# Level products of a linear attention issued alternately for two heads, and one clear for a range of semaphores

## The chip, the cores and the metric

One core of a Trainium2 chip runs the whole kernel. The core has a matrix engine (TensorE, PE in the profile), a vector engine (VectorE, DVE), a scalar engine (ScalarE, ACT), a general engine (GpSimd, POOL) and a queue engine (SyncE, SP), each with its own instruction stream; they meet at semaphores. The metric is the device time in microseconds of one execution, and the median of several executions is compared.

## The reference, cut to what matters

Two layers (DEPTH = 2) of a hybrid model work on two streams of 128 tokens each, a context stream and a sample stream, with 1024 channels. Each layer has a mixing half (gated linear attention with 4 heads, a convolution, a neighbourhood attention) and a mixture of 64 experts. The change touches the gated linear attention. Its part within a chunk is, for tokens i >= j of a chunk:

```
decay = jnp.exp(jnp.where(causal, diff, -jnp.inf))          # diff = bc_i - bc_j, bc = cumsum(log_a)
attn = jnp.sum(q[:, :, :, :, None, :] * k[:, :, :, None, :, :] * decay, axis=-1)
o_intra = jnp.einsum('bhnij,bhnjv->bhniv', attn, v)
```

It is computed forwards and, on the flipped sequence, backwards; both results are added, so each head needs attn for two directions. The head dimension is 64 (DK).

## The kernel before, in words

All weights are streamed from HBM through a ring of four slots; the activations stay in SBUF. The two layers are one hardware loop (`nc.Fori(0, DEPTH)`), whose body has two blocks: a large one with the work of all engines, and a small one in which GpSimd clears semaphores, so that the next pass of the loop can count them from zero again. At the end of a block all engines meet, and after the loop SyncE stores the two outputs.

In the linear attention the token by token matrix of a head is built from seven levels (LEVELS = 7). A level splits the 128 tokens into blocks and takes the products between the late half and the early half of each; scaled by decays relative to the middle of the block, it is one matrix product with 64 rows of contraction. The forward direction has an eighth product, the plain k times q, of which only the diagonal is used. The work is cut into 8 groups g per layer: stream st = g // 4, pair of heads a = g // 2 % 2, direction dr = g % 2. The two heads e = 0 and 1 of a pair lie in partitions 0 to 63 and 64 to 127 of the same tiles. A group goes through the engines like this:

- TensorE, `decays(g)` (L745): the sums of the log decays for the eight levels, into PSUM banks 0 and 1.
- ScalarE (L1136): their exponentials, into a tile E (shown as `h`, two buffers).
- VectorE for group 0, GpSimd for groups 1 to 7, `decayed` (L577, L579): E times q or k, into X (shown as `hT`, one buffer for each direction). It signals `X_ready`.
- TensorE, `pairs(g)` (L760, and L762 for the eighth product): X by X for each level, head 0 into banks 2 and 3, head 1 into banks 6 and 7. It signals `pair_shown` once for each head. A float32 product of the program is two MATMUL and two LDWEIGHTS instructions in the profile, so a head is 14 or 16 of each.
- VectorE, `combine(g)`: for each head a product of the eight (seven) levels with a mask into `tm` (L1353), which signals `masked`, a sum over the levels (L1358 forwards, L1360 backwards), and backwards an addition (L1361), which signals `att_ready`.
- TensorE, `outputs` (L774, L777): attention times v, after each second group.

Before head e of group g, TensorE waits until `masked` shows that VectorE has read the same head of the group before, since the banks are the same. The order on TensorE is written out by hand:

```
for g in range(8):
    pairs(g)
    if ADA_GLA + g < ADA_CHUNKS:
        ada_step(ADA_GLA + g)
    if g + 2 < 8:
        decays(g + 2)
    if g % 2 == 0 and g:
        outputs(g - 1)
outputs(7)
```

`ada_step` (L301, for g = 0, 1, 2) is a product of the modulation weights, with 32 columns of weights per instruction and four such products side by side in the array. After the eight groups follow the chunk states (L797, L799, L804) and the output projection (L812).

The clears are in the second block of the loop body. GpSimd walks over all 144 names and clears all but 15 of them, one instruction each (L1635). The 15 count on through the whole launch.

Of the kernel before, what the change touches and what calls it, by code (L numbers as in the profile page):

```python
# [29 lines left out]
DK = 64  # L30
# [20 lines left out]
LEVELS = 7  # L51
# [59 lines left out]
R_DW, R_DWB, R_LNG, R_LNB, R_ON, R_QN, R_KN, R_END = 0, 31, 32, 33, 34, 35, 36, 37  # L111


SIGNALS = """x_loaded c_loaded const_set const_step matrices c_sig c_step first_in0 first_in1
first_in2 first_in3 first_done first_kept first_bias bias_next small_in vec_in norm_in attn_in shared_in chunk_in0 chunk_in1 chunk_in2
gate_in0 gate_in1 gate_in2 gate_in3 down_in0 down_in1 down_in2 down_in3 act_step dve_step ada_done ada_kept bias_in square_done var_ready
root_ready mod_shown h_ready hT_shown hT_ready vec_shown vec_ready proj_done proj_kept z_shown la_log la_ready
conv_sig tap conv_ready convT_shown ctok_ready convB_shown conv_neg cact_ready pw_shown cat_conv nq_ready
kco_ready nT_shown nT_ready bias_ready scores_shown max_ready p_exp p_ready pT_shown pT_ready pv_shown cat_na
gg_sig decay_shown E_ready X_ready pair_shown masked att_ready o_shown go_ready goT_shown cat_gla st_pre  # L120
st_exp kd_ready st_shown st_kept mix_shown x_mid logits_shown scored g2_shown g2_kept stored y_out hs1 hs2 hs3 ordered tables_shown
tables_kept order_shown sorted_shown order_ready
rest1 rest2 chosen_ready counted places sh_gu sh_silu sh_act sh_turned sh_kept sh_done G_ready
S_ready X_shown X_kept gu_done silu_done act_done turned turn_kept Y_shown Y_kept scattered left_in left_base left_hot left_G left_Xs
# [16 lines left out]
def build(nc, A):  # L141
# [1 line left out]
        return nc.alloc_sbuf_tensor(name, shape, dt)  # L143


    s = {name: nc.alloc_semaphore(name) for name in SIGNALS}


    ring = sb("ring", [P, SLOTS, SLOT])
# [120 lines left out]
    def bank(b, lo=0, hi=512):  # L270
        return ps[:, b, lo:hi]
# [154 lines left out]
    def down(slot, j, half):  # L426
        return slot[:, 2 * KT * FF:SLOT].rearrange("p (j n) -> p j n", j=2)[:, j, 512 * half:512 * (half + 1)]
# [20 lines left out]
    with nc.Block() as block:  # L448
# [137 lines left out]
        def _(pe):  # L586
            mm = nc.tensor.matmul

            def show(n, st, b):

                for c in range(4):
                    last = mm(bank(b, P * c, P * (c + 1)), pick[:, c, st, :], ada[:, n, :], start=True, stop=True)  # L592
                return last
# [36 lines left out]
            for u, (c, c0, w, by_channel, st) in enumerate(UNITS_IN):  # L630
# [7 lines left out]
                for kt in range(KT):  # L638
                    if by_channel:
                        last = mm(ps[0:w, b, 0:STREAMS * P], wt[:, kt, :], hT[:, kt, :],  # L640
                                  start=(kt == 0), stop=(kt == KT - 1))
                    else:
                        last = mm(bank(b, 0, w), hT[:, kt, P * st:P * (st + 1)], wt[:, kt, :],  # L643
                                  start=(kt == 0), stop=(kt == KT - 1))
                last.then_inc(s["proj_done"], 1)
                if u == 3:
# [3 lines left out]
                    for c in range(2):  # L650
                        last = nc.tensor.transpose(bank(5, 64 * c, 64 * c + R_END), vec[:, P * c:P * (c + 1)],
                                                   ident[0:R_END, 0:R_END])
# [10 lines left out]
            for st in range(STREAMS):  # L663
                for c in range(2):
                    at = 256 * st + P * c
                    last = nc.tensor.transpose(bank(4, at, at + P), cacc[:, c, st, :], ident[:])
# [4 lines left out]
            for c in range(2):  # L671
                for st in range(STREAMS):
                    at = 256 * c + P * st
                    last = nc.tensor.transpose(bank(5, at, at + P), cTok[:, st, P * c:P * (c + 1)], ident[:])
# [4 lines left out]
            for o in range(2):  # L679
                for c in range(2):  # L680
                    last = mm(bank(4, 256 * o, 256 * (o + 1)), wpw[:, c, P * o:P * (o + 1)],
                              cacc[:, c, :, :].rearrange("p s t -> p (s t)"), start=(c == 0), stop=(c == 1))
# [10 lines left out]
            for a in range(PAIRS):  # L693
                last = nc.tensor.transpose(bank(6, P * a, P * (a + 1)), kvc[:, 0, P * a:P * (a + 1)], ident[:])
# [5 lines left out]
            for e in range(2):  # L700
                r = slice(DK * e, DK * (e + 1))
                for a in range(PAIRS):
                    last = mm(bank(2 + e, P * a, P * (a + 1)), qnT[r, a, 0:P], knT[r, a, 0:P], start=True, stop=True)
            last.then_inc(s["scores_shown"], 1)
            for e in range(2):
                r = slice(DK * e, DK * (e + 1))
                for a in range(PAIRS):
# [3 lines left out]
                    last = mm(bank(6 + e, 256 * a + P, 256 * (a + 1)), qnT[r, a, P:2 * P], kcT[r, a, :],  # L711
                              start=True, stop=True)
# [8 lines left out]
            for i, block_in in enumerate(blocks):  # L721
                last = nc.tensor.transpose(bank(i // 4, P * (i % 4), P * (i % 4 + 1)), block_in, ident[:])
# [3 lines left out]
            for e in range(2):  # L726
                for a in range(PAIRS):
# [6 lines left out]
                    last = mm(out1, kvc[:, 1, DK * hh:DK * (hh + 1)], pT[:, HEADS + 2 * i + 1, :],  # L734
                              start=False, stop=True)
# [13 lines left out]
            def pairs(g):  # L749

                st, a, dr = g // 4, g // 2 % 2, g % 2
                pe.wait_ge(s["X_ready"], g + 1)
                for e in range(2):
                    if g:
                        pe.wait_ge(s["masked"], 2 * (g - 1) + e + 1)
                    r = slice(DK * e, DK * (e + 1))
                    for lv in range(LEVELS + (dr == 0)):
                        out = bank((2, 6)[e] + lv // 4, P * (lv % 4), P * (lv % 4 + 1))
                        if lv < LEVELS:
                            last = mm(out, X[r, dr, lv, :], X[r, dr, lv, :], start=True, stop=True)  # L760
                        else:
                            last = mm(out, kT[r, a, P * st:P * (st + 1)], qT[r, a, P * st:P * (st + 1)],  # L762
                                      start=True, stop=True)
                    last.then_inc(s["pair_shown"], 1)

            def outputs(g):
                st, a = g // 4, g // 2 % 2
# [17 lines left out]
# [8 lines that stand above are left out]
# [5 lines left out]
            for dr in range(2):  # L798
                last = mm(bank(3, 256 * dr, 256 * (dr + 1)), suf[:, dr, :], la[:, 0, dr, :], start=True, stop=True)  # L799
            last.then_inc(s["st_pre"], 1)  # L800
            pe.wait_ge(s["kd_ready"], 1)
            for dr in range(2):
                for hh in range(HEADS):
                    last = mm(ps[0:DK, 6 + dr, DV * hh:DV * (hh + 1)], kd[:, dr, DK * hh:DK * (hh + 1)],  # L804
                              v[:, 0, DV * hh:DV * (hh + 1)], start=True, stop=True)
# [16 lines left out]
            for st in range(STREAMS):  # L822
                pe.wait_ge(s["go_ready"], st + 1)
                for hh in range(HEADS):
                    last = nc.tensor.transpose(bank(st, P * hh, P * (hh + 1)), gg[:, st, P * hh:P * (hh + 1)], ident[:])
# [13 lines left out]
            for st in range(STREAMS):  # L839
                for kt in range(KT):  # L840
                    last = mm(bank(2 + 4 * st, 0, EXPERTS), hT[:, kt, P * st:P * (st + 1)], wr[:, kt, :],
                              start=(kt == 0), stop=(kt == KT - 1))
                last.then_inc(s["logits_shown"], 1)
            for st in range(STREAMS):
                for half in range(2):
                    last = show(10 + half, st, G2_BANKS[2 * st + half])
# [17 lines left out]
            for st in range(STREAMS):  # L864
                last = mm(ps[0:EXPERTS, 2, 192:192 + EXPERTS], sel[:, st, :], ones[:, 0:EXPERTS], start=(st == 0),
                          stop=(st == STREAMS - 1))
# [5 lines left out]
            for st2 in range(STREAMS):  # L872
                nc.tensor.transpose(ps[0:EXPERTS, 6, P * st2:P * (st2 + 1)], place[:, st2, :], ident[:])
                last = nc.tensor.transpose(ps[0:EXPERTS, 6, P * (2 + st2):P * (3 + st2)],
                                           gate[:, st2, :], ident[:])
# [6 lines left out]
            for a in range(4):  # L882
                last = mm(bank(7, EXPERTS * a, EXPERTS * (a + 1)), tables[:, a, :], order, start=True, stop=True)
# [56 lines left out]
            for st in range(STREAMS):  # L940
                pe.wait_ge(s["sh_act"], st + 1)
                a_in = acts[:, st, :].rearrange("t (p j) -> t j p", j=2)
                for j in range(2):
                    last = nc.tensor.transpose(bank(4 + st, P * j, P * (j + 1)), a_in[:, j, :], ident[:])
# [3 lines left out]
            for st in range(STREAMS):  # L948
                pe.wait_ge(s["sh_kept"], st + 1)
                for half in range(2):  # L950
                    for j in range(2):
                        last = mm(bank(2 * st + half), sh_actT[:, st, P * j:P * (j + 1)], down(shared, j, half),
                                  start=(j == 0), stop=False, skip_group_check=True)
# [674 lines left out]
    with nc.Block() as block:  # L1628
        @block.gpsimd
        def _(pool):  # L1630
            for name in SIGNALS:
                if name not in ("stored", "const_step", "x_loaded", "c_sig", "c_step", "y_out", "c_loaded", "const_set",
                                "first_in0", "first_in1", "first_in2", "first_in3", "first_done", "first_kept",
                                "first_bias"):
                    pool.sem_clear(s[name])  # L1635
    layers.__exit__(None, None, None)


# [33 lines left out]
```

## Time and profile before

| what | us |
|---|---|
| median of 3 runs | 1714.33 |
| lowest, highest | 1712.02, 1715.88 |
| the profiled execution, its own time | 1718.69 |
| its span, from the first to the last instruction | 1717.1 |
| TensorE busy | 1497.6 |
| VectorE busy | 447.6 |
| ScalarE busy | 294.0 |
| GpSimd busy | 149.5 |

The profiled execution took 1.6 us more than its span and lies 4.4 us above the median. Busy time of TensorE is that of overlapping instructions in a pipeline, so it says that something was in the engine, and not that it ran at its peak. The granted clock of TensorE has two levels, shown as 1.00 (2.4 GHz) and 0.50 (1.2 GHz); a stretch with a number between them had both.

### The profile page before, as it was taken

How to read it: one execution, taken by the hardware profiler on the slowest of the kernel's cores; microseconds unless marked ns; L12 is line 12 of the kernel's file. 1: busy time of each engine (PE TensorE's matmuls, PEld its weight loads, DVE VectorE, ACT ScalarE, POOL GpSimd, SP SyncE). 2: the span in 40 equal slices, each digit the busy share in tenths (PEclk: the TensorE clock that was granted, in tenths of full speed). 3: DMA queues.
4: the chain of work that ended last, by engine and by line, in shares of the span. 5: the costliest groups of instructions: out<-in, count | busy, mean ns of one | idle time of the engine just before them, and what ended most of it. 6: DMA issues, size and time to landing. Idle time of an engine off the chain costs nothing. (4 is left out here: it accounts for less than half of the span.)

```text
span 1717.1 us, 28427 instructions
## 1 busy us (share of the span) xinstructions
PE 1497.6 (87%) x12120; PEld 797.8 (46%) x12121; DVE 447.6 (26%) x874; ACT 294.0 (17%) x489; POOL 149.5 (9%) x349
## 2 busy tenths in 40 slices
PE   4897889889898999899659879889899898999994
PEld 3655665634343344344246557564334343334431
DVE  1261684511111111111115219561111111111111
ACT  1313203500010101011023231251001010111110
POOL 3550240000000000000004106000000000000000
PEclk7998989899999999999969999889999999999997
DMA  7648910389999999999554594007999898989992
GB/s 253 228 134 313 334 58 6 139 339 419 367 422 389 421 390 391 390 421 403 215 185 171 175 386 184 7 1 292 403 406 384 368 413 362 416 365 392 404 421 105
DMA packets 109252, 509.56 MB, mean 297 GB/s; under 512 B 12864, under 2 KB 14652, under 8 KB 59196
## 3 DMA queue, kind: packets, MB, share of 16 engines
q1 hardware_dynamic: 108508, 506.52, 73.9%
q8 instruction: 101, 1.65, 0.4%
q0 software_dynamic: 384, 1.05, 0.3%
q14 instruction: 35, 0.29, 0.0%
q10 hardware_dynamic: 224, 0.06, 0.0%
HBM read 505.49 MB, written 2.10 MB: 296 GB/s over the span
## 5 line engine op out<-in xcount | busy, mean ns | idle before, releaser
L907 PE MATMUL ps<-ring,h 128*32 128x512 f32 x3328 | 394.4, 629 | 74.7 <-DMA ring<-in_exp_w_up 45.9
L907 PEld LDWEIGHTS ps<-ring,h 128*32 128x32 f32 x3328 | 118.2, 115 | 345.5 <-issue 345.3
L926 PE MATMUL ps<-ring,mid 128*32 128x512 f32 x1664 | 200.1, 598 | 3.1 <-DVE hT L1515 1.6
L933 PE MATMUL ps<-hT,mid 128*128 128x512 f32 x416 | 192.4, 605 | 1.6 <-DVE hT L1523 1.6
L893 PEld LDWEIGHTS ps<-tm,mid 128*128 128x128 bf16 x2496 | 144.4, 98 | 44.3 <-issue 43.1
L893 PE MATMUL ps<-tm,mid 128*128 128x128 bf16 x2496 | 156.9, 219 | 0.3
L1513 DVE TENSOR_TENSOR mid<-mid,ps 128x256 f32<-128x256 f32 x52 | 21.9, 421 | 470.4 <-ACT mid L1206 470.4
L933 PEld LDWEIGHTS ps<-hT,mid 128*128 128x128 f32 x416 | 74.7, 189 | 120.0 <-issue 116.5
L1515 DVE COPY hT<-ps 128x512 f32<-128x512 f32 x52 | 36.0, 691 | 329.0 <-PE ps L926 329.0
L1206 ACT ACTIVATE mid<-ps 128x256 f32<-128x256 f32 x52 | 19.9, 383 | 541.6 <-PE ps L907 541.6
L301 PE MATMUL ps<-ring,cs 128*32 128x128 f32 x1792 | 65.5, 309 | 46.7 <-DMA ring<-in_w_ada 46.7
L1604 POOL TENSOR_TENSOR ring<-ring,maskr 128x512 f32<-128x512 f32 x2 | 45.2, 22578 | 688.7 <-DMA ring<-in_cache_na_v 688.7
L643 PE MATMUL ps<-ring,hT 128*128 128x512 f32 (+1 forms) x256 | 96.5, 539 | 0.0
L1191 ACT COPY h<-ps 128x512 f32<-128x512 f32 x104 | 60.8, 585 | 177.5 <-PE ps L893 177.5
L301 PEld LDWEIGHTS ps<-ring,cs 128*32 128x32 f32 x1792 | 56.5, 125 | 53.0 <-DMA ring<-in_w_ada 38.9
L926 PEld LDWEIGHTS ps<-ring,mid 128*32 128x32 f32 x1664 | 43.6, 109 | 77.8 <-issue 64.0
L592 PE MATMUL ps<-ada,pick 128*128 128x128 f32 x384 | 52.3, 300 | 30.1 <-issue 18.4
L640 PE MATMUL ps<-hT,ring 128*128 128x256 f32 (+1 forms) x288 | 68.5, 400 | 2.2 <-ACT hT L1041 2.2
L643 PEld LDWEIGHTS ps<-ring,hT 128*128 128x128 f32 x256 | 48.6, 190 | 46.7 <-issue 45.0
L577 POOL TENSOR_TENSOR hT<-h,mid 128x64 f32<-128x64 f32 x196 | 57.3, 329 | 141.2 <-ACT h L1136 141.2
L592 PEld LDWEIGHTS ps<-ada,pick 128*128 128x128 f32 x384 | 51.0, 215 | 36.1 <-issue 30.0
L1208 ACT COPY mid<-ps 128x512 f32<-128x512 f32 x52 | 30.5, 586 | 186.1 <-PE ps L920 186.1
(276 smaller groups left out, 1256.9 us busy)
## 6 DMA issues: line engine op xcount, KB each, us to landing
ring<-in_exp_w_gate SPq DMA_DIRECT2D x128, 1024.0 KB, 10.5
ring<-in_exp_w_up SPq DMA_DIRECT2D x128, 1024.0 KB, 12.8
ring<-in_exp_w_down SPq DMA_DIRECT2D x128, 1024.0 KB, 13.8
ring<-in_w_ada SPq DMA_DIRECT2D x28, 2048.0 KB, 12.9
ring<-in_w_in SPq DMA_DIRECT2D x6, 2048.0 KB, 9.8
ring<-in_w_out SPq DMA_DIRECT2D x4, 2048.0 KB, 7.7
ring<-in_w_in SPq DMA_DIRECT2D x2, 3072.0 KB, 10.5
ring<-in_w_in SPq DMA_DIRECT2D x2, 2176.0 KB, 9.9
```

The source lines that it names most:

```text
L301: last = nc.tensor.matmul(out[32 * c:32 * (c + 1), :], cs[:, kt, :], w[:, kt, P * c:P * (c + 1)], start=(kt == 0), stop=(kt == KT - 1))
L577: last = tt(*views, ALU.mult)
L592: last = mm(bank(b, P * c, P * (c + 1)), pick[:, c, st, :], ada[:, n, :], start=True, stop=True)
L640: last = mm(ps[0:w, b, 0:STREAMS * P], wt[:, kt, :], hT[:, kt, :], start=(kt == 0), stop=(kt == KT - 1))
L643: last = mm(bank(b, 0, w), hT[:, kt, P * st:P * (st + 1)], wt[:, kt, :], start=(kt == 0), stop=(kt == KT - 1))
L893: last = mm(bank(X_bank, P * k, P * (k + 1)), hs[:, part, st, KT // 2 * half + k, :], onehot[:, st], start=(st == 0 and part == 0), stop=( ...
L907: last = mm(ps[first:first + TILE, 4, :], X_e[:, b, kt, first:first + TILE], gate_up(ring[:, slot, :], kt), start=(kt == 0), stop=(kt == K ...
L926: last = mm(ps[first:first + TILE, 7, :], turn[:, P * j + first:P * j + first + TILE], down(ring[:, slot, :], j, half), start=(j == 0), st ...
L933: last = mm(bank(2 * st + half), turn[:, FF + P * st:FF + P * (st + 1)], Y[:, 512 * half:512 * (half + 1)], start=False, stop=False, skip_ ...
L1191: return nc.scalar.copy(X_e[:, b, KT // 2 * half:KT // 2 * (half + 1), :], bank(6).rearrange("p (k n) -> p k n", n=P))
L1515: nc.vector.tensor_copy(Y[:, 0:512], bank(7)).then_inc(s["Y_kept"], 1)
L1604: nc.gpsimd.tensor_tensor(biasr, biasr, maskr[:].unsqueeze(1).broadcast_to([P, HEADS, P]), ALU.add)\
```

## The change

`pairs(g)` takes level by level and in each level head 0 and then head 1, where it took all levels of head 0 and then all of head 1. It waits once, for both heads of the group before, where it waited for each head ahead of its products. Head 0 is signalled behind its last product, which is the last but one of the group. The names of the 15 lasting semaphores are a list of their own, allocated first; the other 129 then have numbers in one unbroken range, and one instruction clears the range.

```diff
-    s = {name: nc.alloc_semaphore(name) for name in SIGNALS}
+    s = {name: nc.alloc_semaphore(name) for name in LASTING + SIGNALS}
+    numbers_of = [s[name].num for name in SIGNALS]
+    per_layer = range(min(numbers_of), max(numbers_of) + 1)
+    assert len(per_layer) == len(SIGNALS)
...
                 pe.wait_ge(s["X_ready"], g + 1)
-                for e in range(2):
-                    if g:
-                        pe.wait_ge(s["masked"], 2 * (g - 1) + e + 1)
-                    r = slice(DK * e, DK * (e + 1))
-                    for lv in range(LEVELS + (dr == 0)):
+                if g:
+                    pe.wait_ge(s["masked"], 2 * g)
+                for lv in range(LEVELS + (dr == 0)):
+                    for e in range(2):
+                        r = slice(DK * e, DK * (e + 1))
                         out = bank((2, 6)[e] + lv // 4, P * (lv % 4), P * (lv % 4 + 1))
                         if lv < LEVELS:
                             last = mm(out, X[r, dr, lv, :], X[r, dr, lv, :], start=True, stop=True)
                         else:
                             last = mm(out, kT[r, a, P * st:P * (st + 1)], qT[r, a, P * st:P * (st + 1)],
                                       start=True, stop=True)
-                    last.then_inc(s["pair_shown"], 1)
+                        if lv == LEVELS - (dr != 0):
+                            last.then_inc(s["pair_shown"], 1)
...
         def _(pool):
-            for name in SIGNALS:
-                if name not in ("stored", "const_step", "x_loaded", "c_sig", "c_step", "y_out", "c_loaded", "const_set",
-                                "first_in0", "first_in1", "first_in2", "first_in3", "first_done", "first_kept",
-                                "first_bias"):
-                    pool.sem_clear(s[name])
+            pool.sem_clear(per_layer)
```

## Rows read from the trace of the kernel before

**Rows 1.** The page: span and busy time of TensorE.

```profile
span 1717.1 us, 28427 instructions
PE 1497.6 (87%) x12120; PEld 797.8 (46%) x12121; DVE 447.6 (26%) x874; ACT 294.0 (17%) x489; POOL 149.5 (9%) x349
```

**Rows 2.** The clears, first layer and second: count, ns min/median/max, first and last start.

```profile
L1635 POOLq EVENT_SEMAPHORE_RANGE_CLEAR  x129: 37/38/47, 858.7 to 867.3; - x129
...
L1635 POOLq EVENT_SEMAPHORE_RANGE_CLEAR  x129: 37/38/47, 1703.9 to 1712.2; - x129
```

**Rows 3.** Timeline around the two ends of a layer: start, us, engine, line.

```profile
857.03 1.23 DVE L1558 TENSOR_TENSOR x<-x,tm 128x1024 f32<-128x1024 f32 x1
871.46 1.28 ACT L1034 ACT_TABLE_LOAD   x1 [27.55 <-issue]
...
1702.22 1.23 DVE L1558 TENSOR_TENSOR x<-x,tm 128x1024 f32<-128x1024 f32 x1
1712.73 0.36 SPq L1642 DMA_DIRECT2D out_y_prompt<-x  x1
```

**Rows 4.** The meeting after the clears, line L1636: ns, first and last start.

```profile
L1636 POOLq ALU_OP  x2: 35/40/45, 867.6 to 1712.5; - x2
...
L1636 PEldq COMPARE_BRANCH  x2: 79/1902/3724, 867.8 to 1712.8; - x2
```

**Rows 5.** Timeline, groups 0 and 1 of the first layer, TensorE and VectorE.

```profile
191.78 1.90 PE L760 MATMUL ps<-hT 64*128 64x128 f32 x16 [0.22 <-DVE hT L577]
...
193.52 0.27 PE L760 MATMUL ps<-hT 64*128 64x128 f32 x1
...
193.53 0.27 PE L762 MATMUL ps<-mid 64*128 64x128 f32 x1
193.63 1.39 PE L760 MATMUL ps<-hT 64*128 64x128 f32 x11
193.90 1.22 DVE L1353 TENSOR_TENSOR tm<-ps,maskf 128x1024 f32<-128x1024 f32 x1 [2.27 <-PE ps L762]
...
195.17 1.95 PE L301 MATMUL ps<-ring,cs 128*32 128x128 f32 x64
...
198.97 3.05 PE L760 MATMUL ps<-hT 64*128 64x128 f32 x28
...
200.90 1.09 DVE L1353 TENSOR_TENSOR tm<-ps,maskb 128x896 f32<-128x896 f32 x1 [0.46 <-PE ps L760]
```

**Rows 6.** What VectorE's L1353 waited for (us, times), then timeline, second layer's group 0.

```profile
  PE ps L762: 5.0, 4
  PE ps L760: 2.7, 4
...
1030.13 1.22 DVE L1353 TENSOR_TENSOR tm<-ps,maskf 128x1024 f32<-128x1024 f32 x1 [2.27 <-PE ps L762]
```

**Rows 7.** Timeline, groups 3 to 5 of the first layer.

```profile
218.82 1.09 DVE L1353 TENSOR_TENSOR tm<-ps,maskb 128x896 f32<-128x896 f32 x1
...
222.24 1.22 DVE L1353 TENSOR_TENSOR tm<-ps,maskf 128x1024 f32<-128x1024 f32 x1
...
225.50 1.23 DVE L1353 TENSOR_TENSOR tm<-ps,maskf 128x1024 f32<-128x1024 f32 x1
...
226.78 1.83 PE L760 MATMUL ps<-hT 64*128 64x128 f32 x14 [0.47 <-DVE tm L1353]
...
228.53 1.98 PE L745 MATMUL ps<-mb,mid 128*128 128x512 f32 x4
228.75 1.09 DVE L1353 TENSOR_TENSOR tm<-ps,maskb 128x896 f32<-128x896 f32 x1
```

**Rows 8.** Timeline, group 7; then windows (clock, DMA share, GB/s last).

```profile
239.92 3.35 PE L760 MATMUL ps<-hT 64*128 64x128 f32 x14 [1.35 <-DVE tm L1353]
...
238.00:240.00 2.00, 0.65 (x7) 0.46 (x5) 1.93 (x3) 0.00 (x0) 0.00 (x0) 0.92 0.00 0
...
256.00:258.00 2.00, 2.00 (x9) 1.35 (x8) 0.00 (x0) 0.91 (x1) 0.00 (x0) 0.81 0.00 0
```

More of the change, by code:

```diff
@@ L111 @@
 R_DW, R_DWB, R_LNG, R_LNB, R_ON, R_QN, R_KN, R_END = 0, 31, 32, 33, 34, 35, 36, 37
-SIGNALS = """x_loaded c_loaded const_set const_step matrices c_sig c_step first_in0 first_in1
-first_in2 first_in3 first_done first_kept first_bias bias_next small_in vec_in norm_in attn_in shared_in chunk_in0 chunk_in1 chunk_in2
+LASTING = """stored const_step x_loaded c_sig c_step y_out c_loaded const_set first_in0 first_in1 first_in2 first_in3
+first_done first_kept first_bias""".split()
+SIGNALS = """matrices bias_next small_in vec_in norm_in attn_in shared_in chunk_in0 chunk_in1 chunk_in2
 gate_in0 gate_in1 gate_in2 gate_in3 down_in0 down_in1 down_in2 down_in3 act_step dve_step ada_done ada_kept bias_in square_done var_ready
@@ L120 @@
 gg_sig decay_shown E_ready X_ready pair_shown masked att_ready o_shown go_ready goT_shown cat_gla st_pre
-st_exp kd_ready st_shown st_kept mix_shown x_mid logits_shown scored g2_shown g2_kept stored y_out hs1 hs2 hs3 ordered tables_shown
+st_exp kd_ready st_shown st_kept mix_shown x_mid logits_shown scored g2_shown g2_kept hs1 hs2 hs3 ordered tables_shown
 tables_kept order_shown sorted_shown order_ready
```

## The prediction

> **What bounds the kernel now.** I read the page first: the span is 1717.1 us and TensorE has something in it for 87% of that [rows 1]. This share says little of the change, which touches two short stretches of each layer. So I read those, each by its own view.
>
> The first is the end of a layer. The timeline has VectorE's last instruction at 857.03 for 1.23, so to 858.26, and the next work of any kind at 871.46, 13.2 us later; after the second layer it is 1703.45 to 1712.73, 9.3 us [rows 3]. The line of the clears fills this: 129 instructions from 858.7 to 867.3, and again from 1703.9 to 1712.2 [rows 2]. The meeting of the engines (L1636) follows at 867.6 and 1712.5 [rows 4]. Nothing runs beside the clears, so they are on the path in full. What remains of the first gap is the jump back to the start of the loop: the longer of TensorE's two branches on L1636 takes 3.72 us [rows 4], and the change leaves it.
>
> The second is the linear attention. The reader is to see who waits for whom in the timeline. VectorE's first mask product starts at 193.90, when head 0 of group 0 is there; in group 1 it waited 0.46 us for TensorE [rows 5]. The sum over both layers is 5.0 and 2.7, together 7.7 us; 2.27 of it in each layer is the first wait, before any product is there [rows 5, 6]. That leaves 7.7 - 4.5 = 3.2 us in which VectorE, in mid-chain, waited for a level product. From group 3 on it has no idle time noted before its mask products, and TensorE waits for VectorE (0.47 at 226.78) [rows 7]. So VectorE sets the pace here, at 6.8 us for a group (219.91 to 226.73, the ends of two second-head masks) [rows 7]. A faster TensorE can win 3.2 us in all, no more; a later one costs at once.
>
> **The clears.** 867.3 - 858.7 = 8.6 us and 1712.2 - 1703.9 = 8.3 us lie between the first and the last clear, 16.9 us together [rows 2]. The instruction that remains is of the same kind: the profile calls the single ones RANGE_CLEAR already, of 38 ns each, at a distance of 8.3 / 128 = 0.065 us. The unknown is what a range of 129 costs. Below, it is one instruction, and 16.9 us go. Above, it walks through its numbers: at 38 ns each that is 4.9 us a layer, 9.8 us back; at the old distance it would be all 16.9. I take the low end, since the same operation is nearest: -16.9. The clears may also have covered a fetch of instructions for what follows; the nearest row is the 3.7 us branch, which stands behind the clears uncovered as it is, so I put this at zero, with 3.7 us a layer as the upper end.
>
> **The alternation, if the two heads overlap.** 16 matmuls of one head take 1.90 us, the last of them 0.27, so they start (1.90 - 0.27) / 15 = 0.109 us apart [rows 5]. Do matmuls of different heads run at once? No row has a whole group in this order. But at the switch between heads in group 0, one of head 1 starts at 193.52 and one of head 0 at 193.53 [rows 5]: 0.01 apart, each with its own weights, into different banks. And the 64 instructions of L301, issued in turn over four column parts, start (1.95 - 0.27) / 63 = 0.027 us apart, a quarter of 0.109 [rows 5]. I take full overlap: a group then needs 1.9 us, not 3.5, and head 0 is complete in the same slot as when it ran alone.
>
> The Trainium skill (TensorE: Matmul & The Clock Gate, "LDWEIGHTS (loading the stationary operand)") speaks against: the load time goes by the 128 columns, whatever the rows. If loads of the two heads queued for one path, nothing would overlap, and the sum would be that of the first rival. Its Part 3 lets loads overlap where row groups differ, and the pair at 193.52 agrees with that.
>
> Now the wait. Both heads start behind the second mask of the group before. Call its end T. TensorE starts at T + 0.05 (226.73 to 226.78) [rows 7]. From the start of a group to VectorE's mask product is 1.93 us with seven levels (198.97 to 200.90) and 2.12 with eight (191.78 to 193.90) [rows 5], so head 0 is usable at T + 1.98 and T + 2.17. VectorE comes free for it at T + 2.02 behind a forward group (226.73 to 228.75) and T + 2.33 behind a backward one (219.91 to 222.24) [rows 7]. The sum over levels hides the products, by 0.04 and 0.16 us. The cover is thin, so I don't take all of the 3.2 us: 0.1 us at some 12 of the 14 later groups stays, and the term is -2.0 (from 0 to -3.2).
>
> Behind the waiting instruction are ada_step, decays(g+2) and outputs on TensorE, and behind them ScalarE and GpSimd. They are not later: they stood behind the same mask, that of the second head, before, with one head's products (1.8 us) still to come, and now two heads' in the same time.
>
> **TensorE's clock.** This is the cost I did not expect at first. Before, a group gave TensorE two bursts of products and one of decays (1.98), with a short pause such as 0.47 [rows 7]. After, from group 3 on, it has 1.9 + 2.0 us of work, at times 0.5 more, in 6.8, then a pause of 2.4 to 2.9 us directly ahead of the next products; ahead of group 7, which has no decays before it, about 3.3. The granted clock fell from 1.00 to 0.50 in the slice from 238 to 240, around a pause of 1.35 ahead of group 7's head 1, and came back only in that from 256 to 258 [rows 8]. So the clock can fall here, ahead of groups 4 to 7. At 1.2 GHz the 14 products of a head take 3.35 us [rows 8] against 1.83 [rows 7]: +1.5, uncovered, while before this befell only head 1 of group 7, behind 2 us of other work. Groups 0 to 3 have the 2 us of an ada_step or short pauses. At most 4 groups x 2 layers x 1.5 = 12 us; at least 0. The pauses lie between one that the clock did not mind (0.47) and more than twice the one around which it fell, yet before it fell once a layer only. I take half: +6.
>
> **Sum:** -16.9 - 2.0 + 6.0 = -12.9 us. The profiled execution's own 1718.69 (span 1717.1 and 1.6 around it) becomes 1705.8. It lies 4.4 above the median of 1714.33, and the same difference gives 1701.4.
>
> **Rivals.** (1) *The heads don't overlap.* Against it stands the pair at 193.52; for it, that only two or so of a group's slots are seen doubled. Head 0's last product would then come 14 slots later with eight levels, 1.52 us, and 12 with seven, 1.30. VectorE waits 1.52 in group 0, 2.17 + 1.52 - 2.33 = 1.36 in the three other forward groups, 1.98 + 1.30 - 2.02 = 1.26 in the four backward ones: 10.6 a layer, 21.2 in all, in place of the 3.2. With -16.9 that is +1.1: 1715.4. If group 7 is at 1.2 GHz its slots double, about 3.3 more a layer: 1722, slower. It decides where head 0 comes 1.2 us late per group or more.
>
> (2) *The clear walks its range.* +9.8 on the forecast: 1711.2. For it, nothing but that no row has a wide range.
>
> (3) *The clock holds.* No +6: 1695.4; with every wait gone 1694.2. (4) *It falls ahead of all eight groups.* +6 more, and the waits stay: 1709.4.
>
> (5) *A fetch comes out from behind the clears.* Up to 7.4: 1708.8.
>
> **How the numbers follow.** Overlap and a cheap clear, with the clock anywhere between (3) and (4), 0.78; rival 1, 0.12, of it two thirds slower; rival 2, 0.06, on the border; rival 5, 0.04. The range from 1694 to 1709 is that of (3) to (4), with some 0.8 in it. A change within 0.2% (3.4 us) can't be told from none here. Faster by more: 0.78 + 0.04 + half of 0.06 = 0.85; within, 0.07; slower, 0.08.
>
> **What the profile will show.** One RANGE_CLEAR a layer, about 0.04 us, and gaps of 4.6 and 1.0 us where 13.2 and 9.3 were. Starts of head 0 and head 1 in pairs, a group's 32 matmuls in about 2 us; at 3.5 rival 1 holds. VectorE's waits for L760 and L762 beyond the first 2.27 under 1 us a layer at clock 1.00, and waits of 1.5 us exactly where the clock is 0.50. The forecast is wrong if the clear is long, if the pairs don't coincide, or if the clock falls never or always.

## The result, and the profile after

| what | before | after |
|---|---|---|
| median, us | 1713.17 (4 runs) | 1692.01 (4 runs) |
| lowest, highest | 1710.96, 1715.88 | 1689.78, 1698.42 |
| the profiled execution, its own time | 1718.69 | 1698.42 |
| its span | 1717.1 | 1696.8 |

The ratio is 0.9882, with a 95% interval from 0.985 to 0.9914: 20 us faster, between 15 and 26. The forecast was 12.9 us faster, and the median lies 2 us below its range. Two repeats of the same kernel gave 0.9902 (0.9883 to 0.9921) and 0.9894 (0.987 to 0.9917), so about 17 to 18 us. Among the runs of the experiments below, one execution of one_wait (3825 us) and two of the kernel before (2224 and 1987 us) were far slower than all others of the same kernel; they are left out of the ratios and of one_wait's median.

The clears first. These are the rows of the page, of the line of the clear and of the branch behind it, which answer to [rows 1, 2, 4], then those of the timeline at the two ends of a layer, which answer to [rows 3].

```profile
span 1696.8 us, 28171 instructions
PE 1480.1 (87%) x12120; PEld 781.1 (46%) x12121; DVE 446.0 (26%) x874; ACT 293.9 (17%) x489; POOL 149.8 (9%) x349
...
L1637 POOLq EVENT_SEMAPHORE_RANGE_CLEAR  x2: 740/740/740, 862.3 to 1691.2; - x2
...
L1638 PEldq COMPARE_BRANCH  x2: 79/1790/3500, 863.5 to 1692.4; - x2
```

```profile
860.57 1.22 DVE L1564 TENSOR_TENSOR x<-x,tm 128x1024 f32<-128x1024 f32 x1
866.98 1.28 ACT L1040 ACT_TABLE_LOAD   x1 [19.54 <-issue]
...
1689.50 1.23 DVE L1564 TENSOR_TENSOR x<-x,tm 128x1024 f32<-128x1024 f32 x1
1692.41 0.36 SPq L1644 DMA_DIRECT2D out_y_prompt<-x  x1
```

A clear takes 0.74 us and not 0.04. The gap from 861.79 to 866.98 is 5.2 us where it was 13.2, that from 1690.73 to 1692.41 is 1.7 where it was 9.3: 8.0 and 7.6 us less, together 15.6. The longer branch at the end of the loop body takes 3.50 us, where it took 3.72.

Next the level products: TensorE in the timeline of the first layer, groups 0, 1, 4, 5, 6 and 7.

```profile
193.54 1.83 PE L765 MATMUL ps<-hT 64*128 64x128 f32 x28 [0.23 <-DVE hT L582]
195.17 0.42 PE L767 MATMUL ps<-mid 64*128 64x128 f32 x4
...
200.31 1.83 PE L765 MATMUL ps<-hT 64*128 64x128 f32 x28 [0.93 <-DVE tm L1359]
...
219.84 3.33 PE L765 MATMUL ps<-hT 64*128 64x128 f32 x28 [2.61 <-DVE tm L1359]
222.90 0.63 PE L767 MATMUL ps<-mid 64*128 64x128 f32 x4
...
228.18 1.83 PE L765 MATMUL ps<-hT 64*128 64x128 f32 x28 [2.30 <-DVE tm L1359]
...
234.52 1.83 PE L765 MATMUL ps<-hT 64*128 64x128 f32 x28 [2.59 <-DVE tm L1359]
...
241.28 3.36 PE L765 MATMUL ps<-hT 64*128 64x128 f32 x28 [3.18 <-DVE tm L1359]
```

28 matmuls in 1.83 us, where 28 took 3.05 [rows 5]: the heads run side by side, (1.83 - 0.27) / 27 = 0.058 us apart. The pause ahead of the products is 0.2 to 0.9 us in the early groups and 2.3 to 3.2 from group 4 on, and in groups 4 and 7 the same 28 take 3.33 and 3.36 us. In groups 5 and 6 they take 1.83 us, behind pauses of 2.30 and 2.59 us, so the pause alone does not decide it. The windows say why; they answer to [rows 8], and the third number from the end is the clock.

```profile
218.00:220.00 2.00, 0.16 (x2) 0.19 (x4) 1.90 (x4) 0.29 (x1) 1.80 (x7) 0.98 0.92 389
220.00:222.00 2.00, 2.00 (x20) 2.00 (x22) 1.97 (x2) 0.00 (x0) 2.00 (x8) 0.50 0.03 8
222.00:224.00 2.00, 2.00 (x18) 1.61 (x16) 0.42 (x2) 0.00 (x0) 0.93 (x3) 0.67 0.00 0
224.00:226.00 2.00, 1.88 (x8) 0.97 (x6) 1.97 (x2) 0.53 (x1) 0.00 (x0) 1.00 0.00 0
...
254.00:256.00 2.00, 0.52 (x2) 0.11 (x1) 0.75 (x3) 0.60 (x1) 0.00 (x0) 0.99 0.00 0
```

The clock falls as group 4's products start, and is back within 4 us. VectorE pays for it: these are its waits of over 0.2 us for a level product, first layer and then second (the 2.27 of the second layer's first group is not shown), and below them the sums over both layers, which answer to [rows 6].

```profile
195.66 1.23 DVE L1359 TENSOR_TENSOR tm<-ps,maskf 128x1024 f32<-128x1024 f32 x1 [2.27 <-PE ps L767]
...
223.58 1.23 DVE L1359 TENSOR_TENSOR tm<-ps,maskf 128x1024 f32<-128x1024 f32 x1 [1.58 <-PE ps L767]
...
244.71 1.09 DVE L1359 TENSOR_TENSOR tm<-ps,maskb 128x896 f32<-128x896 f32 x1 [1.61 <-PE ps L765]
...
1051.27 1.23 DVE L1359 TENSOR_TENSOR tm<-ps,maskf 128x1024 f32<-128x1024 f32 x1 [0.75 <-PE ps L767]
...
1065.36 1.23 DVE L1359 TENSOR_TENSOR tm<-ps,maskf 128x1024 f32<-128x1024 f32 x1 [0.96 <-PE ps L767]
...
1073.37 1.09 DVE L1359 TENSOR_TENSOR tm<-ps,maskb 128x896 f32<-128x896 f32 x1 [1.62 <-PE ps L765]
...
  PE ps L767: 8.2, 7
  PE ps L765: 3.2, 2
```

The waits of 0.46 in group 1 and their like are gone, and five of 0.75 to 1.62 us have come. In sum 11.4 - 4.5 = 6.9 us behind the two first waits, where it was 3.2: +3.7. And yet the stage as a whole did not get longer. I measure it from VectorE's first mask product to the mean square of the second stream behind the attention (L542 before, L547 after): in the first layer from 193.90 to 265.46, which is 71.6 us, and now from 195.66 to 266.42, 70.8. In the second it is 71.6 and 71.2 us. The products of the chunk states behind the groups show part of it, before and after:

```profile
253.54 3.51 PE L804 MATMUL ps<-mid,ring 128*64 128x128 f32 x16 [1.54 <-DVE ring L1371]
...
265.46 0.17 DVE L542 TENSOR_SCALAR sm<-sm 128x4 f32<-128x4 f32 x1
```

```profile
256.06 1.96 PE L810 MATMUL ps<-mid,ring 128*64 128x128 f32 x16 [1.54 <-DVE ring L1377]
...
266.42 0.17 DVE L547 TENSOR_SCALAR sm<-sm 128x4 f32<-128x4 f32 x1
```

They run at 2.4 GHz now, as the clock is back at 254 and not at 256 to 258 [rows 8]. The part on the prediction shows that this earlier return is not bound to the alternation.

### The profile page after: what moved, and what is told of

Same layout as the page of the kernel before. It is cut to its first block and busy times, and to the rows that moved or that the text cites. A ratio compares the mean times of both kernels' runs of the same rounds, so it can differ in the third digit from the quotient of the medians.

```text
span 1696.8 us, 28171 instructions
## 1 busy us (share of the span) xinstructions
PE 1480.1 (87%) x12120; PEld 781.1 (46%) x12121; DVE 446.0 (26%) x874; ACT 293.9 (17%) x489; POOL 149.8 (9%) x349
## 5 line engine op out<-in xcount | busy, mean ns | idle before, releaser
L306 PE MATMUL ps<-ring,cs 128*32 128x128 f32 x1792 | 69.0, 320 | 44.7 <-DMA ring<-in_w_ada 44.7
## 6 DMA issues: line engine op xcount, KB each, us to landing
ring<-in_w_ada SPq DMA_DIRECT2D x28, 2048.0 KB, 13.2
```

The costliest lines, as they stand in the source:

```text
L306: last = nc.tensor.matmul(out[32 * c:32 * (c + 1), :], cs[:, kt, :], w[:, kt, P * c:P * (c + 1)], start=(kt == 0), stop=(kt == KT - 1))
```

## The experiments

Each has a profile, and each but clear_sizes was timed beside the kernel before on the same chip. In the table the stage is the one defined above, of both layers added, in the one execution that was profiled; in the kernel before it is 143.1 us, in the changed kernel's first profile 142.0.

| kernel | median, us | ratio to before (95%) | stage, us |
|---|---|---|---|
| clear_only | 1695.1 | 0.9905 (0.9887 to 0.9923) | 141.7 |
| alt_only | 1706.8 | 0.9977 (0.9958 to 0.9995) | 139.8 |
| renumber | 1712.1 | 1.0006 (0.9988 to 1.0023) | 143.0 |
| both_again | 1694.0 | 0.9902 (0.9883 to 0.9921) | 142.2 |
| both_third | 1691.5 | 0.9894 (0.987 to 0.9917) | 140.8 |
| one_wait | 1696.7 | 0.9908 (0.9883 to 0.9933) | 145.2 |
| hybrid | 1689.1 | 0.9879 (0.9846 to 0.9911) | 135.7 |
| filler | 1682.3 | 0.9831 (0.9801 to 0.9861) | 135.6 |
| late_decays | 1684.0 | 0.9833 (0.9802 to 0.9864) | 135.9 |
| late_again | 1683.4 | 0.9842 (0.9819 to 0.9866) | 137.3 |
| late_old | 1689.8 | 0.9883 (0.986 to 0.9905) | 143.8 |
| clear_sizes | 1694.2 (one execution) | none | 139.6 |

**clear_only.** The clears as changed, the level products as before.

```diff
-                if g:
-                    pe.wait_ge(s["masked"], 2 * g)
-                for lv in range(LEVELS + (dr == 0)):
-                    for e in range(2):
+                for e in range(2):
+                    if g:
+                        pe.wait_ge(s["masked"], 2 * (g - 1) + e + 1)
+                    for lv in range(LEVELS + (dr == 0)):
...
```

> The one range clear and the new list of lasting semaphores, with the level products in the old order. Theory A (the change is the clears, the alternation is near zero): the profile of the changed kernel has gaps of 9.3 and 1.7 us between the last VectorE instruction and the next work at the two ends of a layer... worked out from VectorE's starts on either side, 8.0 and 7.6 us less than before, so -15.6 us, and this kernel is 15.6 us faster than before, to 2 us. Theory B (the alternation wins several us of its own, also outside its stage): the same -15.6 here, and the rest of the 21 us in the next kernel. Theory C (something beside the clears themselves, such as where code or semaphores lie, moves the time): clearly more than 15.6 here.

The first of the two gaps is 5.2 us, not 9.3; the differences of 8.0 and 7.6 us are right. The kernel is 16.2 us faster (13 to 19), as the gaps say: theory A's 15.6 lies within, and theory C is not needed. Theory B expects the same here.

**alt_only.** The kernel before with the new `pairs(g)`.

```diff
-                for e in range(2):
-                    if g:
-                        pe.wait_ge(s["masked"], 2 * (g - 1) + e + 1)
-                    for lv in range(LEVELS + (dr == 0)):
+                if g:
+                    pe.wait_ge(s["masked"], 2 * g)
+                for lv in range(LEVELS + (dr == 0)):
+                    for e in range(2):
...
```

> The alternation and its single wait, with the 129 single clears. Theory A: between +1 and -3 us, since the waits that it removes (3.2 us) and those that it adds at 1.2 GHz (about 7 us in the profile) and an earlier return of the clock behind the groups nearly cancel. Theory B: -5 us or more. In the profile the pairs start together and the waits of about 1.6 us stand where the granted clock is 0.50.

3.9 us faster, with an interval from 0.9 to 7.2. This is between the two theories. In the profiled execution the stage was 139.8 us, one of the short ones. Of its waits at the low clock one is the 1.6 us expected (1.62) and three are less, 0.42, 0.98 and 1.39. The one of 0.42 is in group 4 of the first layer, where the fall of the clock caught only a part of the products: 28 of them took 2.14 us.

**renumber.** The new order of allocation, but 129 single clears and the old products.

```diff
-            pool.sem_clear(per_layer)
+            for name in SIGNALS:
+                pool.sem_clear(s[name])
```

> Only the semaphore numbers change: the lasting ones are allocated first, and the 129 are cleared one by one in the old order of products. Theories A and B: no difference, within 2 us; a difference here is what two equal programs differ by. Theory C: some us faster.

No difference, which refutes theory C.

**both_again, both_third.** The changed kernel, unaltered.

> The changed kernel once more, on the same chip as its parts. Theory A: 16 to 18 us faster than before, the sum of the two parts, and the 21 us of the first four runs were partly scatter. Theory B: 20 us or more faster.

> The changed kernel again: 16 to 20 us faster than before, the range of its two measurements so far.

16.8 and 18.1 us faster. On the chip of its parts it was 1.1 us faster than clear_only, and it is not clear of it; the alternation is worth little, and these runs do not tell its share from nothing. The two parts alone add up to 16.2 + 3.9 = 20.1 us, which the intervals also allow.

**clear_sizes.** The changed kernel with eight redundant clears of 1 to 96 semaphores.

```diff
             pool.sem_clear(per_layer)
+            for n in (1, 2, 4, 8, 16, 32, 64, 96):
+                pool.sem_clear(range(per_layer[0], per_layer[0] + n))
```

> The changed kernel with eight more clears behind its own, of 1, 2, 4, 8, 16, 32, 64 and 96 semaphores of the same range, so that the profile shows the time of a clear against its length. If the engine walks its range, the times rise in a line from 0.04 us for one to 0.74 for 129, which is 0.0055 us a semaphore; if 0.74 us is what any wide clear costs, they are all near 0.74 but the first. The whole kernel is about 2 x 2 us slower by the first, 2 x 6 by the second.

The line of the added clears (count, then ns min/median/max), in three narrow windows: those of 1 and 2, of 16 and 32, of 64 and 96 semaphores. The last row is the clear of all 129.

```profile
L1639 POOLq EVENT_SEMAPHORE_RANGE_CLEAR  x2: 44/44/45, 860.3 to 860.3; - x2
...
L1639 POOLq EVENT_SEMAPHORE_RANGE_CLEAR  x2: 113/156/200, 860.6 to 860.7; - x2
...
L1639 POOLq EVENT_SEMAPHORE_RANGE_CLEAR  x2: 372/458/545, 861.0 to 861.4; - x2
...
L1637 POOLq EVENT_SEMAPHORE_RANGE_CLEAR  x2: 740/740/740, 859.5 to 1684.9; - x2
```

The time grows in a line with the range, as it would if the clear walks it: 372 - 200 = 172 ns for 32 semaphores more, 545 - 372 = 173 for the next 32, 5.4 ns each. One or two take 44 to 45 ns. From the start of the last VectorE instruction to the end of the span it is now 8.95 us, against 7.30 in the changed kernel, so the eight clears, 1.4 us a layer by themselves, are on the path too.

**one_wait.** The changed kernel, with head 0 and then head 1 behind the one wait.

```diff
-                for lv in range(LEVELS + (dr == 0)):
-                    for e in range(2):
+                for e in range(2):
+                    for lv in range(LEVELS + (dr == 0)):
```

> As the changed kernel, but with the heads one after the other behind the one wait: the wait without the alternation. If both heads run at once in the alternation, then a group costs TensorE 3.5 us again here and VectorE waits 0.1 to 0.9 us in groups 1 to 3 as before or more, while in groups 4 to 7 head 0 is ready as early as in the alternation; the longer burst leaves a shorter pause, so fewer falls of the clock: between 0 and 3 us slower than the changed kernel by the first, 3 us faster by the second if the clock holds. Theory A expects them near equal.

VectorE's waits in its first layer, in the timeline:

```profile
193.71 1.23 DVE L1358 TENSOR_TENSOR tm<-ps,maskf 128x1024 f32<-128x1024 f32 x1 [2.27 <-PE ps L767]
...
200.71 1.09 DVE L1358 TENSOR_TENSOR tm<-ps,maskb 128x896 f32<-128x896 f32 x1 [0.44 <-PE ps L765]
...
207.71 1.22 DVE L1358 TENSOR_TENSOR tm<-ps,maskf 128x1024 f32<-128x1024 f32 x1 [0.20 <-PE ps L767]
...
215.16 1.09 DVE L1358 TENSOR_TENSOR tm<-ps,maskb 128x896 f32<-128x896 f32 x1 [0.88 <-PE ps L765]
```

Behind the first they are 0.44, 0.20 and 0.88 us, in groups 1, 2 and 3. In the kernel before they are 0.46 [rows 5], 0.20 and 0.89. So it is the alternation that removes them. In groups 4 to 7 no wait is left in this layer, with the same one wait ahead of the products: here, with the clock at 2.4 GHz, the wait alone cost nothing. In its second layer the clock fell at 1048.5 for 6.8 us, and the waits there are some 5 us behind the first, which makes the stage the longest of all, 145.2 us. The whole kernel can't be told from the changed one (0.9908 against 0.9882 to 0.9902).

**hybrid.** Groups 0 to 3 alternate behind one wait, groups 4 to 7 go as before.

```diff
+                levels = LEVELS + (dr == 0)
+                if g < 4:
+                    if g:
+                        pe.wait_ge(s["masked"], 2 * g)
+                    order = [(lv, e) for lv in range(levels) for e in range(2)]
+                else:
+                    order = [(lv, e) for e in range(2) for lv in range(levels)]
+                for lv, e in order:
+                    if g >= 4 and lv == 0:
+                        pe.wait_ge(s["masked"], 2 * (g - 1) + e + 1)
...
```

> As the changed kernel, but only groups 0 to 3 alternate, behind one wait; groups 4 to 7 take head 0 and then head 1, each behind its own wait, as before. Theory A (alternation wins TensorE's time where TensorE is late, and loses it where the longer pause lets the clock fall): no fall of the clock ahead of groups 4 to 6, VectorE's waits behind the first one under 0.5 us a layer, and 2 to 4 us faster than the changed kernel. Rival (the falls of the clock come anyway, or their waits are hidden or given back later): no faster than the changed kernel.

What its mask products waited for, both layers:

```profile
  PE ps L773: 4.7, 3
```

4.7 - 4.5 = 0.2 us of waiting is left behind the first. The stage is 135.7 us. But the theory had it that the clock would not fall ahead of groups 4 to 6, and it did fall once in each layer (at 225.6 and 1051.6), where head 0's products lie ahead of time and hide it. So the early products of head 0 help here, and not only the clock. The whole kernel gained less than its stage: the stage is as short as that of late_decays and filler on the same chip, but the medians of those are 5 and 7 us lower, and hybrid's interval takes in the changed kernel's ratio. Where the difference lies was not found.

**late_decays, late_again.** The alternation, and in groups 3 to 6 decays and outputs are held back until VectorE has masked head 0.

```diff
+                if 3 <= g < 7:
+                    pe.wait_ge(s["masked"], 2 * g + 1)
                 if g + 2 < 8:
                     decays(g + 2)
                 if g % 2 == 0 and g:
                     outputs(g - 1)
```

> As the changed kernel, with one wait more: in groups 3 to 6 TensorE holds back decays(g+2) and outputs until VectorE has masked head 0 of the group. Same work, but the pause of 2.6 us ahead of the next products is cut in two. Theory A: the clock stays at 1.00 until group 7 at least, the waits of 0.8 to 1.6 us are gone, and the time is like that of the hybrid. Rival (what counts is the sum of the work in a group, not where the pause lies): the clock falls as before and nothing is won; the held decays may even make X late.

> The alternation with the held decays once more, on the chip of the changed kernel below: 7 us faster than that, from 3.4 us less in each layer's stage, if the clock is the cause; equal if the first measurement of it was scatter of the expert stage.

TensorE in the timeline of late_decays, from the decays of group 3 to the products of group 7 (not all rows), and a window behind them:

```profile
213.62 1.98 PE L750 MATMUL ps<-mb,mid 128*128 128x512 f32 x4 [1.22 <-DVE tm L1361]
216.94 1.83 PE L765 MATMUL ps<-hT 64*128 64x128 f32 x28 [1.33 <-DVE tm L1361]
...
223.67 1.83 PE L765 MATMUL ps<-hT 64*128 64x128 f32 x28 [0.91 <-DVE tm L1361]
...
230.02 1.83 PE L765 MATMUL ps<-hT 64*128 64x128 f32 x28 [1.32 <-DVE tm L1361]
...
236.77 1.83 PE L765 MATMUL ps<-hT 64*128 64x128 f32 x28 [1.75 <-DVE tm L1361]
...
242.00:244.00 2.00, 1.18 (x6) 0.88 (x6) 1.97 (x2) 0.00 (x0) 0.00 (x0) 0.56 0.00 0
```

The same work, the same wait ahead of the products, but each pause of 2.3 to 3.2 us is now two of 0.9 to 1.8, and all level products run at 2.4 GHz. The clock falls only behind those of the last group. The waits behind the first ones are 0.5 us in both layers together (1.0 in the second measurement), and the stage is 135.9 us (137.3 in the second measurement, where the clock stayed low longer in the second layer's tail). Beside both_third on one chip late_again is 8.1 us faster, and the intervals of the two don't meet (0.9866 and 0.987 are their near ends). Their profiled stages differ by 3.5 us in both layers together, half of what the expectation had, and the two profiled executions by 2.7 us in all. So the stage shows 3.5 of the 8.1 us; where the rest lies no profile shows.

**filler.** Two more products of 128x128x512 in each of groups 3 to 6, which nobody reads.

```diff
+                if 3 <= g < 7:
+                    b = 5 if g < 6 else 0
...
+                    for _ in range(2):
+                        mm(bank(b), la[:, 0, 0, 0:P], mf[:, 0:4, :].rearrange("p l n -> p (l n)"), start=True, stop=True)
```

> As the changed kernel, with two more 128x128x512 products in each of groups 3 to 6, whose results nobody reads, behind the decays and outputs: 1.7 us of work in the pause. The outputs are unchanged. Theory A: clock at 1.00 up to group 7's products, VectorE's waits beyond the first under 0.5 us a layer, 2 to 4 us faster than the changed kernel though it does more. Rival: no change, or slower by the added work if it reaches the path.

More work in the pauses and the same gain: no fall of the clock until the level products of the last group are done, 0.2 us of waits behind the first ones, and a stage of 135.6 us. The pauses ahead of the products of groups 4 to 7 in its first layer are 0.7 to 1.5 us.

**late_old.** The held decays with the old order of the heads and its two waits.

```diff
+                if 3 <= g < 7:
+                    pe.wait_ge(s["masked"], 2 * g + 1)
                 if g + 2 < 8:
                     decays(g + 2)
```

> One clear, the old order of heads with its two waits, and decays and outputs of groups 3 to 6 held back as in the kernel before this one. If the hold alone is what keeps the clock, the linear attention stage of a layer is about 1.5 us longer than with the alternation (the waits of groups 1 to 3), some 69.5 us from the first mask to the mean square behind it against 67.9, and the kernel is about 3 us slower than late_again. If the alternation is worth nothing once the clock holds, both are equal.

Slower by 6.4 us than late_again on the same chip, more than the 3 expected (the intervals overlap by a little, from 0.986 to 0.9866), and the stage is longer by 6.5. Its waits are 4.5 us behind the first, against 1.0. In the first layer the hold did not keep the clock, which fell at 223.9 and 237.5, before the last group was done; in the second it stayed until the last group. So neither of the two holds the gain alone.

## Why the prediction was wrong

**The clears** were right in place and off in one bound. The term was -16.9 us with one clear at 0.04 us; it is -15.6, since a clear of 129 takes 0.74 us, twice. Rival 2, that it walks its range, fits what was measured, but at 5.4 ns a semaphore and not at 38. No fetch came out from behind the clears (rival 5): the rest of the gap is 5.2 - 0.7 = 4.5 us, against the 4.6 forecast.

**The overlap** was right. The first rival (no overlap) is refuted by 28 matmuls in 1.83 us. The Trainium skill (TensorE: Matmul & The Clock Gate, "LDWEIGHTS (loading the stationary operand)") sets the load time by the 128 columns, whatever the rows. It does not say that the loads of two heads queue; that was the prediction's reading of it, and the trace is against it, with products of the two heads 0.058 us apart, loads included.

**The step that failed is the last term of the sum, "+6.0",** taken as the whole effect of the clock. I costed each fall where it hurts, at four waits of 1.5 us, and asked nowhere what runs at another clock behind the groups. With the -2.0 for the waits removed, the forecast for the stage was net +4. What the profiles show in its place:

- In the first profile the waits alone came out near that: +3.7, which is 6.5 us at the low clock less 2.8 removed. Five waits of 0.75 to 1.62 us stand ahead of groups 4 and 7 in both layers and of 6 in one. That this is so near +4 is partly luck. The waits behind the two first ones are 6.8 us here, but 4.7, 4.9, 3.3 and 2.4 in alt_only, both_again, both_third and clear_sizes, whose level products are the same, and 3.0 to 3.1 in before, clear_only and renumber: +1.4 on average. A fall often catches only a part of a group's products.
- The groups' tail, from the start of the last addition of a group (L1361 before, L1367 after; 247.87 and 250.72 in the first layer) to the mean square, went from 17.6 to 15.7 us, and in the second layer from 17.6 to 16.0: -3.5. This is the clock that is back earlier, and only in part the alternation's doing. A tail is either 15.6 to 16.1 or 17.4 to 17.8 us long. It is long in three of the ten layers with plain alternation, the first of both_again, both_third and clear_sizes, and short in one of the six without it, the first of clear_only, where the products of the chunk states take 1.96 us against 3.68 in its second. On average the alternation goes with -1.7 for both layers.
- VectorE's own instructions in the groups are 1.4 us shorter: 0.8 of it in the additions, 0.35 us each and not 0.40, and 0.6 in the sums over levels. This is nearly the same in all these profiles, and the forecast had no term for it. Why was not tested. In all fourteen profiles every addition of 0.40 us or more runs for most of its length beside a product of GpSimd, but so do 55 of the 144 of under 0.31 us.

So the stage changed by +3.7 - 3.5 - 1.4 = -1.2 in the first profile and not by +4. Over the five profiles with plain alternation it was 139.6 to 142.2 us, and over the three without it 141.7 to 143.1: +1.4 - 1.7 - 1.4 = -1.7 on average, and the two sets overlap.

One reading of the rows was off as well, without weight in the sum: VectorE has no idle time before its mask products from group 4 on, not from group 3. Its first mask product in group 3 had waited 0.89 us, which is in the 3.2.

**The rest is scatter,** and the range left it out. The sum with the measured terms is -15.6 - 1.2 = -16.8, and the two repeats gave -16.8 and -18.1. The profiles of before and after differ by 20.3. The expert stage, which no edit touches, is 4.4 us shorter in the two layers together, and all else 0.9 longer. From VectorE's ranking of the experts (L1458, L1464) to the last residual addition:

```profile
1161.39 0.25 DVE L1458 TENSOR_SCALAR nax<-wanted,nax 64x64 f32<-64x64 f32 x1
...
1702.22 1.23 DVE L1558 TENSOR_TENSOR x<-x,tm 128x1024 f32<-128x1024 f32 x1
```

```profile
1155.09 0.25 DVE L1464 TENSOR_SCALAR nax<-wanted,nax 64x64 f32<-64x64 f32 x1
...
1689.50 1.23 DVE L1564 TENSOR_TENSOR x<-x,tm 128x1024 f32<-128x1024 f32 x1
```

It is 540.8 us before and 534.4 after in the second layer, but 531.9 and 533.9 in the first; over the other kernels' profiles it runs from 527.7 to 537.3. The two profiled executions alone can't tell scatter from an effect; that it is scatter rests on the repeats and on this spread. A range of 15 us around the forecast held the terms' uncertainty and not this one. What sets it from one execution to the next is open.

## What to carry to other kernels

Serial housekeeping between two blocks was on the path in full here, and cheap to remove: look for stretches in which no engine computes. Making TensorE faster where VectorE sets the pace brought little, and it set the clock at risk, because one longer pause took the place of two short ones. Spreading TensorE's work over the pause, by holding back what is not yet needed, was worth more than the alternation, but only together with it. When a term is put down for a clock, follow it past the waits to whatever else runs at that clock, and look at more than one execution. The kernel to keep is the changed one with the held decays, 27 to 29 us faster than before (ratio 0.9842 and 0.9833).

## What was not expected of the hardware

- A semaphore clear takes 5.4 ns for each semaphore of its range: 44 ns for one, 372 for 64, 740 for 129.
- Float32 matmuls with 64 rows, whose two heads lie in the lower and upper half of the partitions, start 0.058 us apart in turn, against 0.109 in one half, weight loads included.
- With the heads alternating, the clock of TensorE fell to 1.2 GHz as the products behind a pause of 2.61 us began (after, group 4), and stayed at 2.4 GHz when each pause was cut into two of 0.9 to 1.8 us with the same work (late_decays, late_again). But it stayed up behind a pause of 2.59 us in the same layer of after, and in the first layer of late_old it fell behind one of 1.15 us. No rule comes out of these rows.
- The same stretch of work behind the groups came back to 2.4 GHz at different times from one layer to another, with the heads alternating or not: the tail took 15.6 to 16.1 us or 17.4 to 17.8.
